# Hybrid diffusion trunk: the copy of the turned probabilities before both exponentials on ScalarE

## The reference

```python
# differential attention: 8 heads, blocks of 128 queries
s = jnp.einsum('qbhid,bkhid->bhiqk', qb, k).astype(jnp.float32) * scale   # i = 0, 1: two maps per head
p = jax.nn.softmax(s, axis=-1)
a = (p[:, :, 0] - lam * p[:, :, 1]).astype(v.dtype)
o = jnp.einsum('bhqk,bkhd->qbhd', a, v)
...
# gates and lifts of the three branches
g = jax.nn.sigmoid(u_gate).reshape(B, L, N_BRANCH, D_MODEL)
merged = g[:, :, 0] * (y_hy @ w_lift[0]) + g[:, :, 1] * (y_na @ w_lift[1]) + g[:, :, 2] * (y_da @ w_lift[2])
```

## Time and profile before

| what | value |
|---|---|
| median of 3 runs (lowest to highest) | 2916.35 us (2914.2 to 2916.5) |
| the profiled execution's own time | 2910.96 us |
| its span in the trace | 2909.2 us |
| mean granted TensorE clock | 0.974 |
| busy: PE, DVE, ACT, POOL | 95%, 65%, 34%, 49% of the span |
| chain that ended last | PE 74%, DVE 12%, ACT 5% |
| the 40 units in the trace | layer 0 from 651 to 941 us, layer 1 from 1993 to 2280 us |

### The profile page before, as it was taken

The page is one execution under the profiler, slowest core; times in us unless marked ns, Lnnn a source line. Parts: engine busy times, 40 slices in busy tenths (PEclk is TensorE's granted clock), DMA queues, the critical chain, the costliest instruction groups (busy, mean ns, idle before and its releaser), DMA issues.

```text
span 2909.2 us, 43789 instructions
## 1 busy us (share of the span) xinstructions
PE 2760.9 (95%) x17224; PEld 2483.7 (85%) x17224; DVE 1878.3 (65%) x2941; ACT 980.7 (34%) x1843; POOL 1438.2 (49%) x620
## 2 busy tenths in 40 slices
PE   7879899999999998999998989999999998999998
PEld 2348777888888998999997969797988898999998
DVE  6456577674445558888886478565544565855866
ACT  3442112315655115242242112313565213422422
POOL 0425233283433774656665605065434575667554
PEclk9879998999999999999999999899999999999999
DMA  5422243141111432334222216032111331222222
GB/s 224 140 98 90 87 138 131 70 123 39 52 53 46 162 101 95 118 93 124 80 88 83 88 65 229 12 129 85 53 46 45 124 126 59 80 86 75 88 80 80
DMA packets 80537, 275.34 MB, mean 95 GB/s; under 512 B 9003, under 2 KB 14763, under 8 KB 78156
## 3 DMA queue, kind: packets, MB, share of 16 engines
q1 hardware_dynamic: 48124, 168.77, 18.8%
q10 hardware_dynamic: 32208, 103.77, 10.3%
HBM read 248.91 MB, written 23.59 MB: 94 GB/s over the span
## 4 chain that ended last, share of the span: by engine, by line
PE 74%; DVE 12%; ACT 5%; DVEq 4%; DMA 3%; issue 2%; POOLq 0%; POOL 0%; ACTq 0%; SPq 0%
PE PS L606 32%; PE PS L946 9%; PE PS L1086 7%; PE PS L667 4%; PE PS L995 3%; PE PS L741 2%; DVEq L2108 2%; DMA wraw<-in_w_strips 2%; PE PS L893 2%; DVE bsum L2109 2%; PE PS L616 1%; PE PS L967 1%; PE PS L877 1%; PE PS L707 1%; PE PS L829 1%
## 5 line engine op out<-in xcount | busy, mean ns | idle before, releaser
L574 POOL TENSOR_SCALAR whi<-wraw 128x1024 fp32r<-128x1024 f32 x188 | 550.3, 2927 | 982.9 <-PE PS L606 485.7
L576 POOL TENSOR_TENSOR wlo<-wraw,whi 128x1024 fp32r<-128x1024 f32 x212 | 552.8, 2608 | 90.1 <-ACT whi L1375 60.9
L1673 DVE CUSTOM_DVE_ANT_0 adap<-ada,cond 128x1024 f32<-128x1024 f32 x176 | 315.9, 1795 | 32.6 <-DMA ada<-in_w_ada 11.8
L606 PE MATMUL PS<-hhi,whi 128*128 128x320 f32 x1152 | 264.4, 311 | 11.6 <-POOL wlo L576 11.3
L606 PE MATMUL PS<-hlo,whi 128*128 128x320 f32 x1152 | 262.9, 309 | 0.0
L606 PE MATMUL PS<-hhi,wlo 128*128 128x320 f32 x1152 | 262.7, 309 | 0.0
L587 POOL TENSOR_TENSOR blo<-bsum,bhi 128x512 fp32r<-128x512 f32 x120 | 175.9, 1472 | 168.0 <-ACT bhi L1538 168.0
L2067 DVE SCALAR_TENSOR_TENSOR x<-PS,mod,x 128x128 f32<-128x128 f32 (+2 forms) x240 | 90.8, 433 | 177.5 <-PE PS L606 174.9
L606 PEld LDWEIGHTS PS<-hhi,whi 128*128 128x128 f32 x1152 | 192.4, 188 | 14.4 <-POOL wlo L576 12.6
L1086 PE MATMUL PS<-hhi,bhi 128*128 128x320 f32 x640 | 199.3, 311 | 1.6 <-POOL blo L587 1.0
L1086 PE MATMUL PS<-hhi,blo 128*128 128x320 f32 x640 | 197.7, 309 | 0.0
(11 more groups left out here) (335 smaller groups left out, 7276.5 us busy)
## 6 DMA issues: line engine op xcount, KB each, us to landing
wraw<-in_w_strips SPq DMA_DIRECT2D x292, 512.0 KB, 3.6
ada<-in_w_ada ACTq DMA_DIRECT2D x80, 512.0 KB, 4.9
spectra<-hst ACTq DMA_DIRECT2D x48, 256.0 KB, 2.1
cond<-conds ACTq DMA_DIRECT2D x7, 1024.0 KB, 7.2
hld<-spectra ACTq DMA_DIRECT2D x8, 768.0 KB, 5.1
hld<-spectra ACTq DMA_DIRECT2D x12, 512.0 KB, 3.7
part<-hacc ACTq DMA_DIRECT2D x8, 640.0 KB, 3.5
macc<-part ACTq DMA_DIRECT2D x8, 640.0 KB, 4.2
```

What stands on the lines that cost most here:

```text
L574: nc.gpsimd.tensor_scalar(hi, raw, 1.0, None, ALU.mult)
L576: nc.gpsimd.tensor_tensor(lo, raw, hi, ALU.subtract).then_inc(w_split, 1)
L606: ins = pe.matmul(out[:, h, :], w[:, kt, :], mv[:, h * HALF:(h + 1) * HALF], start=start and m == 0, stop=stop and m == 2)
L1673: ins = V.tensor_tensor_reduce(adap[s][:, :], ada[s][j][:, :], cond[s][:, c, :], 1.0, 0.0, ALU.mult, ALU.add, mraw[:, 2 * m + c:2 * m + c ...
```

## The change

In the loop over the iterations ScalarE's order was first exponential of n, copy of n-1, second exponential of n. It becomes copy of n-1, both exponentials of n. Nothing else is changed.

```diff
@@ -1476,11 +1476,10 @@
                 for n in range(41):
-                    if n < 40:
-                        da_exp(n, 0)
                     if n:
                         da_keep(n - 1)
                     if n < 40:
+                        da_exp(n, 0)
                         da_exp(n, 1)
                     ready = halves_in(steps_before(n) + 2 * (steps_before(n + 1) - steps_before(n)) // 3)
                     for e in range(kept, ready):
                         early_sigmoid(e)
                     kept = ready
```

## The result

The changed kernel takes 2944.11 us (median of 4 runs, 2942.34 to 2953.41), the kernel before 2915.27 (median of 4, 2910.96 to 2916.5). The ratio is 1.0103, with a 95% interval of 1.0078 to 1.0128: slower by 29 us. Forecast were 2928.5 and a range that ended at 2942.0, so the sign was right and both the number and the range too low.

A forecast was written before the change was run, and what follows sets the result against it. TensorE, busy 95% of the span, bounds the kernel. Units 8 to 39 +11.8, small units -5.6, clock +6: +12, so 2923 on 2910.96, or 2928.5 on the median 2916.35; +6 to +20 has 0.68, range 2916 to 2942.

The forecast's parts named there:

- The mechanism: ScalarE, units after a sigmoid: Exp's table load falls behind the copy, exponentials end 1.77 us later, five sigmoids hold TensorE.
- 5 x 1.77: Units 17, 22, 27, 32 and 37: TensorE goes on 1.77 us later behind each sigmoid, 8.9 lost per layer.
- The other sigmoids have 1.7 us to spare or more: Sigmoids outside units 17, 22, 27, 32, 37: their delay would be hidden, no new wait of TensorE.
- The small units: First eight units of each layer: product and scores come earlier, 3.7 us less in layer 0, 1.9 in layer 1.
- The copy's gain: Units 8 to 39: earlier copy lets TensorE's product start sooner, 3.0 us gained per layer.
- 22 units x 0.12 + 5 x 0.07: Per layer, units 8 to 39: 0.12 us gained in 22 units, 0.07 in five short ones, 3.0 in sum.
- Of eight pauses over 2 us I take four or five as followed by the low clock: TensorE's pauses at sigmoids, both layers: clock falls to 1.2 GHz behind some, one known already; +6, between 0 and +16.
- Its price is in the trace too: 1.5: One low clock behind a pause costs 1.5 us: around unit 37, layer 1 took 15.20, layer 0 13.70.
- It nearly cancels: No pause is followed by the low clock, copy gains 0.17 us per unit: +4, 2920; chance 0.13.
- The clock falls behind each pause: Eight to ten falls, some for longer, and layer 0's slow start stays: +26, 2942; chance 0.09.
- the third rival: Table load behind the copy takes 1.4 us more, a drain: +50 over the forecast, 2980; chance 0.02.
- needed 2 us or more later by the turn: VectorE's difference comes 1 us later, but the turn needs it only 2 us or more later.

The follow-up runs named there:

- the second and fifth experiments: Second: changed kernel, order of before in units 17, 22, 27, 32, 37, 2904.42 us. Fifth: kernel before, new order in units 0 to 8 alone, 2908.50 us.

## Why the prediction was wrong, point by point

**The mechanism was right.** The load of Exp's table fell behind the copy, the exponentials ended 3.72 after the turn, and the sigmoids of units 17, 22, 27, 32 and 37 held TensorE. The term "5 x 1.77" per layer measured 1.77 or 1.78 in each: unit 17 takes 9.80, 22 10.24, 27 10.68, 32 10.69 and 37 11.13 in the kernel whose pauses are filled, where before they took 8.03, 8.47, 8.91, 8.91 and 9.35. That the first of these would be a new wait was right, too. "The other sigmoids have 1.7 us to spare or more" was too easy, since 1.77 was asked of them: the one of unit 13 has 1.69 (it ended at 718.29, TensorE went on in its bank at 719.98), and unit 13 now takes 8.02 and not 7.78.

**The small units** were forecast to give 3.7 and 1.9, and gave 3.7 and 1.9 (29.76 and 27.93 to 26.05), for the reasons given.

**The copy's gain** was under-sized: "22 units x 0.12 + 5 x 0.07" was worked from the start of the product, while the units show 0.17 to 0.18, the upper bound, and 0.09. Less what units 13, 29 and 34 lose it is 7.7 over both layers, and not 6. Where the array isn't idle, but the weight load is late, the loss seems to be that of the load, which the earlier trace rows had shown (12.3 us over 39 loads, against 4.8 in 5 waits of the matmuls); no run tests that by itself.

**The step that failed is the clock.** "Of eight pauses over 2 us I take four or five as followed by the low clock": all ten were, the 1.77 of unit 17 included. "Its price is in the trace too: 1.5": they cost 24.9 in sum, 2.5 each. The term was +6, with an upper bound of +16; it was 24.9 less the 1.5 that layer 1 had lost before, so +23.4. With this and the copy's gain put right the sum of the prediction becomes 17.7 - 7.7 - 5.6 + 23.4 = +27.8. (The 7.7 is what is left of the +33.4 in units 8 to 38 when the other two terms are taken out, so the sum has to come out. In layer 0 the plain units gave 0.16 to 0.18 each, unit 26 0.25, most short ones 0.08 to 0.09, and unit 21, whose product had waited for late maxima, 0.69.)

The count was taken from all of the trace, where waits of 3.2 us were followed by the low clock or not. The places of this stage behave more evenly: over the changed kernel and the one with the new order in five units, pauses of 2.65 and over were followed by it 12 times in 12, those of 2.2 three times in 4, those of 1.76 twice in 4; those of 1.2 in the kernel before and in the second and fifth experiments 3 times in 12. The price was taken from one case, at 0.89 over 15 us, while unit 23 after the pause ran at 0.73 for 10. That case was a short stretch of low clock. Here it is, and below it the one that follows the pause in unit 22 of the changed kernel:

```profile
2257.52:2260.93 3.41, 3.41 (x14) 3.08 (x14) 1.40 (x5) 0.92 (x1) 0.00 (x0) 0.50 0.02 5
...
801.32:808.14 6.82, 6.82 (x26) 5.60 (x25) 2.20 (x3) 0.00 (x0) 0.00 (x0) 0.50 0.01 2
```

Four of the ten stretches were of 3.4 us, and by the units' times against those with the pauses filled they cost 1.5 to 1.6 each, as forecast. The other six were of 6.8 us and cost 3.1 to 3.2 each; what makes a stretch short or long is not shown. So two things were too low: the count, ten for four or five, and the price of most.

**The rivals.** "It nearly cancels" at +4 needed that no pause is followed by the low clock. With the pauses filled the units take 2.9 more than before and the medians differ by 7: the price was about right, and the case didn't come. (That 2919.7 meets the rival's 2920 is in part luck, since the two stand on different medians of the kernel before, 2912.58 and 2916.35.) "The clock falls behind each pause", given 0.09 and +26, is what came, though its other half (the slow start of layer 0 stays) did not; so that its +26 comes near the 27.8 of the units is in part luck. Of the third rival's drain there is nothing to see: the copy ends at 796.20, the load behind it takes from 796.21 to 797.49, and the exponential starts at 797.50. The Trainium skill gives, in "ScalarE: Activation LUTs", section "What ACT_TABLE_LOAD costs", 1283 ns for a load and about 1380 ns for a drain. By these rows the first holds here, and of the second nothing is seen.

**VectorE** did wait for the late exponentials, in 25 units of layer 0:

```profile
DVE rsum L1968 <- ACT dp L1444: 27.2, 25, 1.3
```

and this cost little. The difference of unit 28 of layer 0 took 2.89 where 0.9 is usual, and the turn waited for it by 0.35:

```profile
857.53 2.89 DVE L1975 SCALAR_TENSOR_TENSOR dp<-dp,coef,dp 128x640 f32<-128x640 f32 x1
...
860.47 0.66 PE L982 MATMUL PS<-ident,dp 128*128 128x128 f32 x4 [0.35 <-DVE dp L1975]
```

It started just behind a GpSimd instruction (L576, 857.36 for 2.38) that it had missed before. With that unit 29 takes 0.57 more than its neighbours; unit 34 loses 0.2 in the same way. In the traces of before and after the difference and that GpSimd instruction overlap 17 times. In the ten where the difference started first it took 0.88 or 0.89; in the seven where GpSimd did, it ended 0.68 us after GpSimd's instruction. The kernel before has four of the seven; one starts at 780.69, at the beginning of unit 21, and maxima, exponential and copy come late behind it. The prediction had said "needed 2 us or more later by the turn"; a difference that takes 2.0 longer uses that up.

## What to carry to other kernels

An activation table load is an instruction in its engine's queue: in these runs it is free only while it stands ahead of a wait, so before an instruction is moved to the front, look at which load it pushes behind its own wait. Where an engine already waits in a trace, delays behind that wait come through in full, and a one-column activation that asks for the table early takes most of them away (1.43 of 1.77), the sigmoid taken while its table is still loaded all. And a pause of TensorE of about 2 us or more has to be priced with the clock behind it, each time, and not at the mildest case in the trace: here the pauses cost 17.7 us and the clock 24.9.

## What the runs showed of the hardware that was not expected

Ten useless matmuls in a wait of TensorE made the kernel faster. In unit 22 they ran for 1.63 us and left 0.73 of 2.21 us of waiting, the granted clock stayed at 1.00 instead of falling to 0.73 in the next unit, and over ten such places (8 to 16 matmuls in each) 24.9 us of the changed kernel's time went away. The Trainium skill says in "TensorE: Matmul & The Clock Gate", section "Why this matters for your kernels", that throughput drops are avoided by leaving no long gaps between bursts of matmuls. The run agrees, and adds that work without a use fills a gap too, and that this already pays at pauses of 1.8 to 3.1 us.

A weight load that is held back seems to cost the product behind it all of its delay although the array still has work: plain units went from 7.95 to 7.77 when their 0.17 us of waiting loads vanished. No run tested that by itself.
